# Router logits from transposed raw rows, and idle TensorE products between the first expert stage and the conv

## The chip, the cores and the metric

The kernel runs on one core of a Trainium2 chip (trn2). The metric is the device time of one execution in microseconds (us), as the median of several runs. TensorE multiplies matrices, VectorE and ScalarE work on vectors, GpSimd issues the indirect DMAs (gathers and scatters of rows), and SyncE issues nearly all other DMAs, in program order. The engines run independently and wait for one another through semaphores.

## The reference: what is computed

One inference step of a two-layer network over T = 544 frames (512 of a new stream, 32 of a running one) of D = 1024 features, all in fp32. Each layer is a mixer and a mixture of experts, each ahead of a residual addition and behind an RMS norm. The mixer of layer 0 is attention plus a gated recurrence, that of layer 1 a short convolution between two projections. The part that the change touches is the mixture's router:

```
def rmsnorm(x, gain):
    y = xf * rsqrt(mean(xf * xf, axis=-1) + RMS_EPS)
    return y * gain
hp = hp + mix_p
hp = hp + hier_moe(rmsnorm(hp, norm_ffn[layer]), w_group, b_group, w_expert, b_expert, w1, w3, w2)
...
g_logits = xt @ w_group + b_group                      # 4 groups
grp      = argmax(g_logits)                            # top-1 group
e_logits = xt @ w_expert + b_expert                    # 32 experts, 8 in a group
topv, topi = top_k(e_logits of grp, 2)                 # top-2 experts in it
h   = silu(xt @ w1[e]) * (xt @ w3[e]) * gate
out = h @ w2[e]
```

The normed row is the raw row times one number of the row (1/rms) times one gain per feature. A logit is a sum over features, so the gain can be multiplied into the router's weights and 1/rms can be applied to the finished sum.

## The kernel before

**Tiling.** The frames lie as five chunks of 128, 128, 128, 128 and 32 rows (`ROWS`) in `H`, one row to a partition, its features along the partition's memory. KT = 8 is the number of 128-feature pieces.

**Stages, in order of time.** Input projection and mixer of layer 0 (to about 299 us); its output projection (`project_out(0, ...)`, L909) to 360 us; the router of layer 0 to about 392 us; its 32 experts to 633 us; combining the experts' rows, the norm and the transposes for the conv to 664 us; the conv (`conv_terms`, L1044) to 813 us; the output projection of layer 1 to 871 us, its router to 901 us, its experts to 1137 us, and the combining and writing of the results to the end.

**Output projection and its additions.** `project_out` runs over four column quarters s and, in each, over the five chunks c, 24 products each. VectorE's `residual` adds each result to `H` (L1621). When the last quarter of a chunk is in, it signals `h_ok`, ScalarE's `square` takes the chunk's sum of squares (L1089) and its root (L1091), and VectorE's `norm` (L1351, L1357) takes the reciprocal into `rstd` and writes H * rstd * gain to `XF`, one chunk behind the additions. For the expert stages the row is written with its features permuted: feature 8q + k goes to column 128k + q, so that piece k is contiguous. Five DMAs (L428) copy `XF` to `x_rows` in DRAM, from which the experts' rows are gathered later.

**Router.** TensorE's `norm_transpose` (L648) transposes each chunk of `XF` in eight 128-column pieces into two PSUM banks: chunks 0, 1 and 2 behind the last quarter's products of chunks 2, 3 and 4, then chunks 3 and 4. ScalarE's `xt_copy` (L1099) copies the banks to `XT`, chunk 4's second half is copied by VectorE's `xt_high` (L1361). The logits (L931) are 16 products, `wr` (the router's weights of one piece, 36 columns) by 256 or 288 frames of `XT`. ScalarE (L1275) and VectorE (L1637) copy them out, TensorE turns them back to one frame a partition (L936), and VectorE adds the bias `biasr` (L1643, L1644). Then follow VectorE's choice of group and experts, products that rank the frames within each expert, the tables, and GpSimd's first gather (L584).

**Idle products.** `idle_products(b, count)` (L627) multiplies the identity by itself into PSUM bank b, count times, and nothing reads the result. Each layer's router has groups of 6, 26, 11 and 22 of them, each in a stretch in which TensorE waits.

**Expert weights.** The weights of an expert are 3 MB. Six sets fit in memory. SyncE loads experts 0 to 2 beside the output projection, experts 3 and 4 when the five `x_rows` writes have landed (`x_out`) and the logits are done (`lg_mm`; expert 3 goes where `XT` lies, experts 4 and 5 where `XN` and `XF` lie), expert 5 when the first two gathers have landed, and each later one when the expert six before it has been used. Experts are computed in pairs (L966, L972, L978, L983), and GpSimd scatters their rows to `y_rows` (L588).

**From layer 0's experts to the conv.** When all scatters have landed, SyncE loads the rows back into `yab` (L467), VectorE's `combine` adds them to `H` (L1791), and squares, norms (now to `XN`, not permuted), transposes (L648), and the split of each value into a high and a low part (`mixer_in_hi`, L1116; `mixer_in_lo`, L1369) follow for chunks 0 to 2. TensorE then starts the first feature block, 48 records in two of three parts, transposes chunks 3 and 4, and goes on with the rest. On its own side TensorE waits, after the last expert, for ScalarE's last copy of a result, reads the largest number of rows of an expert (`value_load`), and branches around a loop for experts with over 64 rows, which isn't taken here.

## Time and profile before

| | |
|---|---|
| median of 3 runs | 1168.28 us (1168.16 to 1169.54) |
| the profiled execution, its own time | 1169.81 us |
| its span | 1168.1 us |
| TensorE busy | 1013.1 us (87%) |
| VectorE, ScalarE, GpSimd busy | 389.6, 307.1, 189.8 us |
| memory traffic | 282.81 MB, mean 242 GB/s |
| chain that ended last | TensorE 64%, DMA 19%, SyncE's issues 9%, VectorE 5% |
| mean granted TensorE clock | 0.936 of full speed |

How to read it: the profile shows one execution, taken by the hardware. PE is TensorE, PEld its weight loads, DVE VectorE, ACT ScalarE, POOL GpSimd, SP SyncE (SPq: its issuing of DMAs). L909 is line 909 of the kernel. An fp32 product can stand as two records, since it is carried out in passes. Times of a row count from the start of the span. The releaser behind an idle time is inferred.

### The profile page before, as it was taken

The page shows a single profiled execution, that of the slowest core. Times are in us where ns is not written, and L with a number is a line of the kernel's source. Part 1 is how long each engine was busy: PE and PEld are TensorE (multiplying, and loading weights), DVE is VectorE, ACT ScalarE, POOL GpSimd, SP SyncE. Part 2 cuts the span into 40 slices and gives each one's busy share as a digit, 9 for nine tenths or more (in the row PEclk, how much of TensorE's full clock was granted, in tenths as well). Part 3 has the DMA queues.
Part 4 walks back from the last instruction along what each step waited for, and adds up shares of the span by engine and source line. Part 5 has one row for each costly group of instructions (what it writes and reads, how often), then busy time and mean ns, then how long its engine had stood idle before and what let it go on. Part 6 is the DMA issues. An engine that isn't in the chain of part 4 may idle for free.

```text
span 1168.1 us, 20266 instructions
## 1 busy us (share of the span) xinstructions
PE 1013.1 (87%) x8635; PEld 793.4 (68%) x8635; DVE 389.6 (33%) x857; ACT 307.1 (26%) x712; POOL 189.8 (16%) x188
## 2 busy tenths in 40 slices
PE   6999999989998899778775499999998999778880
PEld 5999898965897665444442499999996655444440
DVE  5242464257336211101101755546354111001104
ACT  6254344246223122111112421221131121111110
POOL 7344213120000122122111000000001222122110
PEclk9999998989899999989889599999999999899896
DMA  6432121420744999999996624243677999999966
GB/s 223 96 105 82 38 75 60 111 93 2 248 163 195 360 416 416 417 417 415 417 414 205 213 55 109 55 109 144 181 165 282 405 417 416 416 417 416 415 265 240
DMA packets 114724, 282.81 MB, mean 242 GB/s; under 512 B 22814, under 2 KB 69962, under 8 KB 98216
## 3 DMA queue, kind: packets, MB, share of 16 engines
q1 hardware_dynamic: 104904, 263.63, 60.8%
q0 software_dynamic: 9728, 17.85, 4.1%
q8 instruction: 70, 1.15, 0.5%
q14 instruction: 22, 0.18, 0.0%
HBM read 270.54 MB, written 27.02 MB: 255 GB/s over the span
## 4 chain that ended last, share of the span: by engine, by line
PE 64%; DMA 19%; SPq 9%; DVE 5%; issue 2%; ACT 1%; POOL 1%; DVEq 0%; POOLq 0%; ACTq 0%
DMA w<-in_w_dram 15%; PE banks L1044 13%; PE banks L972 10%; PE banks L677 10%; PE banks L909 9%; PE banks L676 6%; SPq L396 6%; PE banks L983 5%; SPq L399 2%; PE banks L648 1%; PE banks L966 1%; DMA yab<-y_rows 1%; PE banks L870 1%; PE banks L854 1%; PE banks L837 1%
## 5 line engine op out<-in xcount | busy, mean ns | idle before, releaser
L972 PE MATMUL banks<-w,xgT 128*64 128x256 f32 x2048 | 261.6, 416 | 65.5 <-DMA w<-in_w_dram 64.3
L972 PEld LDWEIGHTS banks<-w,xgT 128*64 128x64 f32 x2048 | 162.2, 150 | 172.4 <-DMA w<-in_w_dram 72.7
L1729 DVE TENSOR_TENSOR hh<-banks,sg 128x128 f32<-128x128 f32 x64 | 18.7, 292 | 407.0 <-ACT sg L1290 407.0
L588 POOL DMA_INDIRECT y_rows<-ys,yidx x64 | 63.6, 994 | 381.3 <-ACT ys L1298 379.9
L983 PE MATMUL banks<-w,hT 128*64 128x512 f32 x512 | 116.9, 598 | 0.0
L1044 PE MATMUL banks<-xc_hi,wc_hi 128*128 128x272 f32 x384 | 111.5, 290 | 2.1 <-DVE xc_lo L1369 2.1
L1044 PE MATMUL banks<-xc_hi,wc_lo 128*128 128x272 f32 x384 | 111.7, 291 | 0.0
L1044 PE MATMUL banks<-xc_lo,wc_hi 128*128 128x272 f32 x384 | 111.0, 289 | 0.0
L584 POOL DMA_INDIRECT xr<-x_rows,gidx x32 | 33.4, 1045 | 403.6 <-DVE yidx L1715 385.2
L574 POOL TENSOR_TENSOR wab_lo<-wab,wab_hi 128x512 fp32r<-128x512 f32 x56 | 77.0, 1406 | 131.4 <-ACT wab_hi L1104 130.5
L677 PE MATMUL banks<-wab_hi,xc_hi 128*128 128x256 f32 (+1 forms) x320 | 94.4, 295 | 3.8 <-DVE xp_lo L1369 2.1
L1290 ACT ACTIVATE sg<-banks 128x128 f32<-128x128 f32 x64 | 17.8, 278 | 293.0 <-PE banks L972 293.0
L677 PE MATMUL banks<-wab_hi,xp_lo 128*128 128x256 f32 (+1 forms) x320 | 93.0, 291 | 0.0
L677 PE MATMUL banks<-wab_lo,xc_hi 128*128 128x256 f32 (+1 forms) x320 | 90.4, 286 | 0.0
L1044 PEld LDWEIGHTS banks<-xc_hi,wc_hi 128*128 128x128 f32 x384 | 73.0, 190 | 2.6 <-issue 2.5
L983 PEld LDWEIGHTS banks<-w,hT 128*64 128x64 f32 x512 | 34.1, 136 | 58.5 <-issue 54.6
L1044 PEld LDWEIGHTS banks<-xc_lo,wc_hi 128*128 128x128 f32 x384 | 73.0, 190 | 0.0
L1044 PEld LDWEIGHTS banks<-xc_hi,wc_lo 128*128 128x128 f32 x384 | 72.8, 190 | 0.0
L1298 ACT ACTIVATE ys<-banks 128x512 f32<-128x512 f32 x64 | 38.2, 597 | 97.9 <-PE banks L983 97.9
L677 PEld LDWEIGHTS banks<-wab_hi,xc_hi 128*128 128x128 f32 (+1 forms) x320 | 58.3, 182 | 5.1 <-issue 4.2
L677 PEld LDWEIGHTS banks<-wab_hi,xp_lo 128*128 128x128 f32 (+1 forms) x320 | 58.3, 182 | 0.4
L677 PEld LDWEIGHTS banks<-wab_lo,xc_hi 128*128 128x128 f32 (+1 forms) x320 | 56.9, 179 | 0.7 <-POOL wab_lo L574 0.3
(284 smaller groups left out, 1762.0 us busy)
## 6 DMA issues: line engine op xcount, KB each, us to landing
w<-in_w_dram SPq DMA_DIRECT2D x192, 1024.0 KB, 23.0
wab<-in_w_in_ab_dram SPq DMA_DIRECT2D x13, 1024.0 KB, 5.1
wc<-in_w_in_c_dram SPq DMA_DIRECT2D x24, 512.0 KB, 5.8
yab<-y_rows SPq DMA_DIRECT2D x16, 512.0 KB, 6.7
wo<-in_w_out_ab_dram SPq DMA_DIRECT2D x4, 1024.0 KB, 7.0
x_rows<-XF SPq DMA_DIRECT2D x8, 512.0 KB, 3.5
wo<-in_w_out_c_dram SPq DMA_DIRECT2D x4, 1024.0 KB, 5.9
H<-in_x_prompt_dram SPq DMA_DIRECT2D x4, 512.0 KB, 8.3
```

The lines of the kernel that those rows point to most:

```text
L396: sp.dma_start(w13[s][:, part, :, :], w[l, bass.ds(e, 1)].rearrange("e (p k) f -> p (e k) f", p=P)).then_inc(done, 16)
L399: sp.dma_start(w2s[s][:], w2[l, bass.ds(e, 1)].rearrange("e (a p) n -> p (e a) n", p=P)).then_inc(done, 16)
L574: last = pool.tensor_tensor(wab_lo[n % 3][:, k:k + 2, :], wab[n % 3][:, k:k + 2, :], wab_hi[n % 3][:, k:k + 2, :].bitcast(F32), ALU.subtract)
L584: pool.indirect_dma_start(xr[i][:, :], None, x_dram[l][:, :], bass.IndirectOffsetOnAxis(ap=index.bitcast(U32), axis=0), bounds_check=T - 1 ...
L588: pool.indirect_dma_start(y_dram[l][:, :], bass.IndirectOffsetOnAxis(ap=index.bitcast(U32), axis=0), ys[i][:, :], None, bounds_check=4 * T ...
L676: return pe.matmul(out, w[:, k, cols], x[:, k, t], **flags)
L677: return pe.matmul(out, x[:, k, t], w[:, k, :], **flags)
L909: last = pe.matmul(bank[i % 4][0:ROWS[c], 0:OW], z(a, k)[:, c * P:c * P + ROWS[c]], w(b, k, s), start=k == 0 and j == 0, stop=k == KT - 1 ...
L972: last = pe.matmul(bank[hb][64 * f:64 * f + 64, 0:2 * P].rearrange("p (w j) -> p w j", w=2), xgT[i][:, k, 64 * ab:64 * ab + 64], w13[s][:, ...
L983: last = pe.matmul(bank[6 + ab][64 * n:64 * n + 64, :], hT[ab][:, 64 * f:64 * f + 64], w2s[s][:, f, n * 512:(n + 1) * 512], start=f == 0, ...
L1044: last = pe.matmul(bank[3 * half + a][:, 0:HALF], w[s][:, k, a, :], x[:, k, half * HALF:(half + 1) * HALF], start=k == 0 and j == 0, stop= ...
L1298: act.activation(ys[e % 4][:], bank[6 + ab][:, :], ACT.Copy).then_inc(ys_ok, 1)
```

## The change

In both layers the router's logits are taken from transposed raw rows. `norm_transpose` with an odd n waits for `h_ok` in place of `xn_ok` and loads columns k, k+8, k+16, ... of `H`. It is moved one chunk forward: chunks 0 to 3 stand behind the products of chunks 1 to 4. The six idle products before chunk 4 are gone. ScalarE makes all the copies to `XT`, and those of chunks 3 and 4 stand ahead of chunk 4's square; VectorE's `xt_high` is gone. VectorE multiplies `wr` by the gains (`gcol`, a new DMA) once a layer, ahead of the first addition. The logits' products run first over the frames of chunks 0 and 1, then over those of chunks 2 to 4, with a signal of their own for the first part. The bias addition becomes a scaled one, by `rstd`, chunk by chunk. SyncE issues expert 3's load when the logits are done, and only expert 4's also waits for the `x_rows` writes. `XF` is still made and written as before. Apart from the router, TensorE runs 140 idle products between layer 0's last expert and the first transposes for the conv, and 10, 4 and 12 behind those of chunks 0, 1 and 2.

```
+        gcol = small("gcol", KT)
...
                 sp.dma_start(wr[:, :, NG:NR], w_expert[l].rearrange("(p k) n -> p k n", p=P)).then_inc(wr_in, 16)
                 sp.dma_start(biasr[:, 0:NG], b_group[l:l + 1, :].partition_broadcast(P)).then_inc(wr_in, 16)
                 sp.dma_start(biasr[:, NG:NR], b_expert[l:l + 1, :].partition_broadcast(P)).then_inc(wr_in, 16)
+                sp.dma_start(gcol[:], norm_ffn[l].rearrange("(p k) -> p k", k=KT)).then_inc(wr_in, 16)
 
 
             wcv = w_in_c[0].rearrange("(k p) (a m n) -> a m p k n", p=P, a=3, n=P)
...
                 for c in range(NC):
                     sp.wait_ge(xn_ok, NC * (2 * l + 1) + c + 1)
                     sp.dma_start(x_dram[l][c * P:c * P + ROWS[c], :], XF[0:ROWS[c], c, :]).then_inc(x_out, 16)
+                sp.wait_ge(lg_mm, 2 * l + 1)
+                first_load(l, 3)
                 sp.wait_ge(x_out, 16 * NC * (l + 1))
-                sp.wait_ge(lg_mm, 2 * l + 1)
-                for j in (3, 4):
-                    first_load(l, j)
+                first_load(l, 4)
                 for i in range(2):
                     sp.wait_ge(xr_in[i], 16 * (PAIRS // 2 * l + 1))
                 first_load(l, 5)
...
                     pe.matmul(bank[b][:, 0:P], ident[:], ident[:], start=True, stop=True)
 
             def norm_transpose(n, c):
-                if n % 2 == 1 and c == 4:
-                    idle_products(1, 6)
-                pe.wait_ge(xn_ok, NC * n + c + 1)
+                if n % 2 == 0:
+                    pe.wait_ge(xn_ok, NC * n + c + 1)
+                else:
+                    pe.wait_ge(h_ok, NC * (n - 1) + c + 1)
                 if n == 0 and c == 0:
                     pe.wait_ge(pool_c, zeroed[0])
 
...
                         pe.wait_ge(xt_a if half == 0 else xt_d, NC * n + c - 1)
                     for kk in range(4):
                         k = 4 * half + kk
-                        last = pe.transpose(bank[low + half][:, kk * P:kk * P + ROWS[c]], (XN, XF)[n % 2][0:ROWS[c], c, k * P:(k + 1) * P],
+                        rows = H[0:ROWS[c], c, k::KT] if n % 2 else XN[0:ROWS[c], c, k * P:(k + 1) * P]
+                        last = pe.transpose(bank[low + half][:, kk * P:kk * P + ROWS[c]], rows,
                                             ident[0:ROWS[c], 0:ROWS[c]])
                     last.then_inc(xt_mm, 1)
 
...
                             last = pe.matmul(bank[i % 4][0:ROWS[c], 0:OW], z(a, k)[:, c * P:c * P + ROWS[c]], w(b, k, s),
                                              start=k == 0 and j == 0, stop=k == KT - 1 and j == 2)
                     last.then_inc(op_mm, 1)
-                    if s == OQ - 1 and c >= 2:
-                        norm_transpose(2 * n + 1, c - 2)
+                    if s == OQ - 1 and c >= 1:
+                        norm_transpose(2 * n + 1, c - 1)
 
             def z_ab(part, k):
                 return ((zA_hi, zA_lo), (zB_hi, zB_lo))[k // 4][part][:, k % 4, :]
...
             project_out(0, z_ab, lambda part, k, s: (wo_hi, wo_lo)[part][0][s][:, k, :], w_lo, 15)
 
             def mixture(l):
-                for c in (3, 4):
-                    norm_transpose(2 * l + 1, c)
-                pe.wait_ge(xt_a, NC * (2 * l + 2))
-                pe.wait_ge(xt_d, NC * (2 * l + 2))
+                norm_transpose(2 * l + 1, NC - 1)
                 pe.wait_ge(op_add, OQ * NC * (l + 1))
-
-                pe.wait_ge(wr_in, 64 * (l + 1))
-                for k in range(KT):
-                    for p0, t in ((0, slice(0, 2 * P)), (64, slice(2 * P, T))):
+                pe.wait_ge(wg_ok, l + 1)
+                for p0, t, chunks, done in ((0, slice(0, 2 * P), 2, lgh_mm), (64, slice(2 * P, T), NC, lg_mm)):
+                    pe.wait_ge(xt_a, NC * (2 * l + 1) + chunks)
+                    pe.wait_ge(xt_d, NC * (2 * l + 1) + chunks)
+                    for k in range(KT):
                         last = pe.matmul(bank[0][p0:p0 + NR, 0:t.stop - t.start], wr[:, k, :], XT[l][:, k, t], start=k == 0, stop=k == KT - 1)
-                last.then_inc(lg_mm, 1)
+                    last.then_inc(done, 1)
                 pe.wait_ge(lgT_ok, 2 * l + 2)
                 for c in range(NC):
                     p0, t0 = (0, c * P) if c < 2 else (64, (c - 2) * P)
...
             def frames_ready(c):
                 pe.wait_ge(xt_a, NC * 2 + c)
                 pe.wait_ge(xt_d, NC * 2 + c)
+            idle_products(2, 140)
             for c in range(3):
                 norm_transpose(2, c)
+                idle_products(2, (10, 4, 12)[c])
             pe.wait_ge(wc_lo_ok, 1)
             frames_ready(3)
             for a in range(3):
...
                 for q in range(1, OQ):
                     out_hi(l, q)
                 for c in range(NC):
+                    if c == NC - 1:
+                        xt_copy(2 * l + 1, c - 1, 0, xt_a)
+                        xt_copy(2 * l + 1, c - 1, 1, xt_d)
+                        xt_copy(2 * l + 1, c, 0, xt_a)
+                        xt_copy(2 * l + 1, c, 1, xt_d)
                     square(2 * l + 1, c)
-                    if c >= 2:
-                        xt_copy(2 * l + 1, c - 2, 0, xt_a)
-                        xt_copy(2 * l + 1, c - 2, 1, xt_d)
-                xt_copy(2 * l + 1, 3, 0, xt_a)
-                xt_copy(2 * l + 1, 3, 1, xt_d)
-                xt_copy(2 * l + 1, 4, 0, xt_a)
-                act.wait_ge(lg_mm, 2 * l + 1)
+                    if 0 < c < NC - 1:
+                        xt_copy(2 * l + 1, c - 1, 0, xt_a)
+                        xt_copy(2 * l + 1, c - 1, 1, xt_d)
+                act.wait_ge(lgh_mm, l + 1)
                 act.activation(lgT[0:NR, 0:2 * P], bank[0][0:NR, 0:2 * P], ACT.Copy).then_inc(lgT_ok, 1)
                 act.wait_ge(ge_ok, 2 * l + 1)
                 act.activation(rt[3][:, :, 0:NG], rt[3][:, :, 0:NG], ACT.Exp).then_inc(ex_ok, 1)
...
-
-            def xt_high(n, c):
-                dve.wait_ge(xt_mm, NXT * n + 2 * c + 2)
-                dve.tensor_copy(XT[n // 2][:, 4:8, c * P:c * P + ROWS[c]],
-                                bank[7 - 2 * (c % 2)][:, :].rearrange("p (k t) -> p k t", k=4)[:, :, 0:ROWS[c]]).then_inc(xt_d, 1)
...
 
             def residual(n):
 
+                dve.wait_ge(wr_in, 80 * (n + 1))
+                dve.tensor_tensor(wr[:], wr[:], bc(gcol[:].unsqueeze(2), [P, KT, NR]), ALU.mult).then_inc(wg_ok, 1)
                 for i in range(OQ * NC):
                     s, c = divmod(i, NC)
                     dve.wait_ge(op_mm, OQ * NC * n + i + 1)
...
                         if c > 0:
                             norm(2 * n + 1, c - 1)
                 norm(2 * n + 1, NC - 1)
-                xt_high(2 * n + 1, NC - 1)
             residual(0)
 
             def route(l):
...
                 dve.wait_ge(lg_mm, 2 * l + 1)
                 dve.tensor_copy(lgT[64:64 + NR, :], bank[0][64:64 + NR, 0:T - 2 * P]).then_inc(lgT_ok, 1)
                 dve.wait_ge(lg_mm, 2 * l + 2)
-                dve.wait_ge(wr_in, 64 * (l + 1))
                 z = [b[:, 0:NC * NR].rearrange("p (c n) -> p c n", c=NC) for b in (bank[2], bank[3])]
-                for i in range(2):
-                    c2 = slice(2 * i, 2 * i + 2)
-                    tie(dve.tensor_tensor(lg[:, c2, :], z[i][:, c2, :], bc(biasr[:].unsqueeze(1), [P, 2, NR]), ALU.add))
-                dve.tensor_tensor(lg[0:DEC, 4, :], z[1][0:DEC, 4, :], biasr[0:DEC, :], ALU.add).then_inc(lg_ok, 1)
+                for c in range(NC):
+                    n = ROWS[c]
+                    last = dve.scalar_tensor_tensor(lg[0:n, c, :], z[c // 2 if c < 4 else 1][0:n, c, :], rstd[0:n, c:c + 1], biasr[0:n, :], ALU.mult, ALU.add)
+                last.then_inc(lg_ok, 1)
                 dve.wait_ge(lg_ok, l + 1)
 
                 def first_max(v, w, rev, eq, key, hot, top):
```

On TensorE, the end of layer 0's output projection up to its router's first idle products. `wo_*` and `z*` are operands of the projection, `lgT` are the logits with the frames along the columns. Before:

```order
L909 MATMUL banks<-wo_lo_3_191,zB_hi 32x256
L648 MATMUL banks<-ident,XF 128x128 x16
L627 MATMUL banks<-ident 128x128 x6
L648 MATMUL banks<-ident,XF 128x32 x8
L931 MATMUL banks<-XT_104,wr 36x256
L931 MATMUL banks<-XT_104,wr 36x288
...
L936 MATMUL banks<-ident,lgT 128x36 x4
L936 MATMUL banks<-ident,lgT 32x36
L627 MATMUL banks<-ident 128x128 x26
```

And with the change:

```order
L913 MATMUL banks<-wo_lo_3_192,zB_hi 32x256
L652 MATMUL banks<-ident,H 128x128 x8
L652 MATMUL banks<-ident,H 128x32 x8
L933 MATMUL banks<-XT_105,wr 36x256 x8
L933 MATMUL banks<-XT_105,wr 36x288 x8
L938 MATMUL banks<-ident,lgT 128x36 x4
L938 MATMUL banks<-ident,lgT 32x36
L629 MATMUL banks<-ident 128x128 x26
```

One chunk's transposes are left behind the last product where two were (the other chunk's, and so each earlier one's, has moved a product forward), they read `H`, and six idle products are gone.

On ScalarE, the same place, from the square of chunk 2 to the copy of the logits (`junk,ssq` and `rms` are a chunk's square and root). Before:

```order
L1089 ACTIVATE junk,ssq<-H 128x1024
L1091 ACTIVATE rms<-ssq,epsc 128x1
L1099 ACTIVATE XT_104<-banks 128x4x128 x2
L1089 ACTIVATE junk,ssq<-H 128x1024
L1091 ACTIVATE rms<-ssq,epsc 128x1
L1099 ACTIVATE XT_104<-banks 128x4x128 x2
L1089 ACTIVATE junk,ssq<-H 128x1024
L1091 ACTIVATE rms<-ssq,epsc 128x1
L1099 ACTIVATE XT_104<-banks 128x4x128 x4
L1099 ACTIVATE XT_104<-banks 128x4x32
L1275 ACTIVATE lgT<-banks 36x256
```

And with the change, from the square of chunk 3:

```order
L1093 ACTIVATE junk,ssq<-H 128x1024
L1095 ACTIVATE rms<-ssq,epsc 128x1
L1103 ACTIVATE XT_105<-banks 128x4x128 x4
L1103 ACTIVATE XT_105<-banks 128x4x32 x2
L1093 ACTIVATE junk,ssq<-H 128x1024
L1095 ACTIVATE rms<-ssq,epsc 128x1
L1281 ACTIVATE lgT<-banks 36x256
```

The copies of the last chunks have moved ahead of chunk 4's square and root.

On TensorE, between the branch behind layer 0's experts and the conv. Before:

```order
L1021 COMPARE_AND_BRANCH
L1021 UNCONDITIONAL_BRANCH
L648 MATMUL banks<-ident,XN 128x128 x24
L1044 MATMUL banks<-xc_hi,wc_hi_265 128x272
L1044 MATMUL banks<-xc_lo,wc_hi_265 128x272
```

And with the change:

```order
L1023 COMPARE_AND_BRANCH
L1023 UNCONDITIONAL_BRANCH
L629 MATMUL banks<-ident 128x128 x140
L652 MATMUL banks<-ident,XN 128x128 x8
L629 MATMUL banks<-ident 128x128 x10
L652 MATMUL banks<-ident,XN 128x128 x8
L629 MATMUL banks<-ident 128x128 x4
L652 MATMUL banks<-ident,XN 128x128 x8
L629 MATMUL banks<-ident 128x128 x12
L1046 MATMUL banks<-xc_hi,wc_hi_266 128x272
```

Nothing is moved here; 166 products are put in, in TensorE's own order.

## Rows read from the trace of the kernel before

**Rows 1.** the page, section 2: memory traffic in 40 equal slices of the span

```profile
GB/s 223 96 105 82 38 75 60 111 93 2 248 163 195 360 416 416 417 417 415 417 414 205 213 55 109 55 109 144 181 165 282 405 417 416 416 417 416 415 265 240
```

**Rows 2.** windows around the first gather: busy per engine, TensorE clock, DMA share, GB/s

```profile
390.00:392.00 2.00, 0.37 (x3) 0.37 (x4) 0.00 (x0) 0.00 (x0) 0.00 (x0) 1.00 0.30 113
394.00:396.00 2.00, 2.00 (x22) 1.60 (x19) 0.00 (x0) 0.22 (x1) 0.48 (x1) 1.00 0.94 385
```

**Rows 3.** chain of waits, end of the output projection: start us, us, what

```profile
356.23 0.87 PE banks L648 x8
357.10 2.79 PE banks L909 x24
```

**Rows 4.** timeline of TensorE, layer 0's router: start us, us, line, operation [idle before]

```profile
363.64 2.73 PE L627 MATMUL banks<-ident 128*128 128x128 f32 x12
366.31 0.99 PE L648 MATMUL banks<-ident,XF 32*128 32x32 f32 x8
367.72 4.08 PE L931 MATMUL banks<-XT,wr 128*36 128x256 f32 x32 [0.43 <-ACT XT L1099]
```

**Rows 5.** timeline of VectorE, the same stretch

```profile
349.10 0.42 DVE L1621 TENSOR_TENSOR H<-banks,H 128x256 f32<-128x256 f32 x1 [2.43 <-PE banks L909]
...
359.91 0.41 DVE L1621 TENSOR_TENSOR H<-banks,H 32x256 f32<-32x256 f32 x1 [0.78 <-PE banks L909]
...
362.72 2.03 DVE L1357 SCALAR_TENSOR_TENSOR XF<-H,rstd,gffn 128x1024 f32<-128x1024 f32 x1
...
371.91 0.46 DVE L1637 COPY lgT<-banks 36x288 f32<-36x288 f32 x1 [4.10 <-PE banks L931]
372.82 0.50 DVE L1643 TENSOR_TENSOR lg<-banks,biasr 128x72 f32<-128x72 f32 x2 [0.45 <-PE banks L936]
```

**Rows 6.** timeline of ScalarE, the same stretch

```profile
358.17 1.07 ACT L1099 ACTIVATE XT<-banks 128x512 f32<-128x512 f32 x2
360.41 1.06 ACT L1089 ACTIVATE junk<-H 128x1024 bf16<-128x1024 f32 x1 [1.18 <-DVEq L1626]
...
361.59 0.29 ACT L1091 ACTIVATE rms<-ssq,epsc 128x1 f32<-128x1 f32 x1
```

**Rows 7.** timeline of VectorE, layer 1's router

```profile
871.26 0.41 DVE L1621 TENSOR_TENSOR H<-banks,H 32x256 f32<-32x256 f32 x1 [0.78 <-PE banks L909]
...
881.72 0.46 DVE L1637 COPY lgT<-banks 36x288 f32<-36x288 f32 x1 [4.10 <-PE banks L931]
```

**Rows 8.** timeline of GpSimd, the first gather of layer 0

```profile
385.98 1.20 POOL L584 DMA_INDIRECT xr<-x_rows,gidx  x1 [124.98 <-DVE yidx L1715]
```

**Rows 9.** timeline of TensorE: two groups of idle products in layer 0's router

```profile
372.71 6.07 PE L627 MATMUL banks<-ident 128*128 128x128 f32 x52
...
379.74 2.70 PE L627 MATMUL banks<-ident 128*128 128x128 f32 x22
```

**Rows 10.** timeline, all engines, from layer 0's last expert to the conv

```profile
635.20 2.76 ACT L1314 ACTIVATE wc_hi<-wc 128x3072 fp32r<-128x3072 f32 x1 [1.46 <-DMA wc<-in_w_in_c_dram]
...
654.32 1.97 PE L648 MATMUL banks<-ident,XN 128*128 128x128 f32 x8 [21.23 <-DVE XN L1357]
...
662.81 1.29 DVE L1369 TENSOR_TENSOR xc_lo<-banks,xc_hi 128x512 fp32r<-128x512 f32 x2 [0.42 <-ACT xc_hi L1116]
...
671.14 1.28 DVE L1357 SCALAR_TENSOR_TENSOR XN<-H,rstd,gmix 128x1024 f32<-128x1024 f32 x1
```

**Rows 11.** chain of waits, start of the conv

```profile
664.25 7.73 PE banks L1044 x48
...
673.46 139.09 PE banks L1044 x1104
```

**Rows 12.** a window in that stretch, columns as in rows 2

```profile
636.00:640.00 4.00, 0.00 (x0) 0.00 (x0) 2.00 (x1) 1.96 (x1) 0.00 (x0) 0.59 1.17 316
```

**Rows 13.** groups by form, VectorE, 374 to 376 us: count | busy, mean ns | idle

```profile
L1661 DVE TENSOR_REDUCE rt<-rt 128x40 f32<-128x160 f32 x1 | 0.4, 433 | 0.0
L1659 DVE TENSOR_TENSOR rt<-lg,rt 128x160 f32<-128x160 f32 x1 | 0.3, 318 | 0.0
```

More of the change, by code:

```diff
@@ L118, in hmoe_step @@
         biasr = small("biasr", NR)
+        gcol = small("gcol", KT)
         row_no = small("row_no", 2 * NC)
@@ L416, in router_load @@
                 sp.dma_start(biasr[:, NG:NR], b_expert[l:l + 1, :].partition_broadcast(P)).then_inc(wr_in, 16)
+                sp.dma_start(gcol[:], norm_ffn[l].rearrange("(p k) -> p k", k=KT)).then_inc(wr_in, 16)
             wcv = w_in_c[0].rearrange("(k p) (a m n) -> a m p k n", p=P, a=3, n=P)
@@ L428, in mixture @@
                     sp.dma_start(x_dram[l][c * P:c * P + ROWS[c], :], XF[0:ROWS[c], c, :]).then_inc(x_out, 16)
+                sp.wait_ge(lg_mm, 2 * l + 1)
+                first_load(l, 3)
                 sp.wait_ge(x_out, 16 * NC * (l + 1))
-                sp.wait_ge(lg_mm, 2 * l + 1)
-                for j in (3, 4):
-                    first_load(l, j)
+                first_load(l, 4)
                 for i in range(2):
@@ L629, in norm_transpose @@
             def norm_transpose(n, c):
-                if n % 2 == 1 and c == 4:
-                    idle_products(1, 6)
-                pe.wait_ge(xn_ok, NC * n + c + 1)
+                if n % 2 == 0:
+                    pe.wait_ge(xn_ok, NC * n + c + 1)
+                else:
+                    pe.wait_ge(h_ok, NC * (n - 1) + c + 1)
                 if n == 0 and c == 0:
@@ L647, in norm_transpose @@
                         k = 4 * half + kk
-                        last = pe.transpose(bank[low + half][:, kk * P:kk * P + ROWS[c]], (XN, XF)[n % 2][0:ROWS[c], c, k * P:(k + 1) * P],
+                        rows = H[0:ROWS[c], c, k::KT] if n % 2 else XN[0:ROWS[c], c, k * P:(k + 1) * P]
+                        last = pe.transpose(bank[low + half][:, kk * P:kk * P + ROWS[c]], rows,
                                             ident[0:ROWS[c], 0:ROWS[c]])
@@ L911, in project_out @@
                     last.then_inc(op_mm, 1)
-                    if s == OQ - 1 and c >= 2:
-                        norm_transpose(2 * n + 1, c - 2)
+                    if s == OQ - 1 and c >= 1:
+                        norm_transpose(2 * n + 1, c - 1)
             def z_ab(part, k):
@@ L921, in mixture @@
             def mixture(l):
-                for c in (3, 4):
-                    norm_transpose(2 * l + 1, c)
-                pe.wait_ge(xt_a, NC * (2 * l + 2))
-                pe.wait_ge(xt_d, NC * (2 * l + 2))
+                norm_transpose(2 * l + 1, NC - 1)
                 pe.wait_ge(op_add, OQ * NC * (l + 1))
-                pe.wait_ge(wr_in, 64 * (l + 1))
-                for k in range(KT):
-                    for p0, t in ((0, slice(0, 2 * P)), (64, slice(2 * P, T))):
+                pe.wait_ge(wg_ok, l + 1)
+                for p0, t, chunks, done in ((0, slice(0, 2 * P), 2, lgh_mm), (64, slice(2 * P, T), NC, lg_mm)):
+                    pe.wait_ge(xt_a, NC * (2 * l + 1) + chunks)
+                    pe.wait_ge(xt_d, NC * (2 * l + 1) + chunks)
+                    for k in range(KT):
                         last = pe.matmul(bank[0][p0:p0 + NR, 0:t.stop - t.start], wr[:, k, :], XT[l][:, k, t], start=k == 0, stop=k == KT - 1)
-                last.then_inc(lg_mm, 1)
+                    last.then_inc(done, 1)
                 pe.wait_ge(lgT_ok, 2 * l + 2)
@@ L1266, in mixture @@
                 for c in range(NC):
[L1267 to L1274 removed]
+                    if c == NC - 1:
+                        xt_copy(2 * l + 1, c - 1, 0, xt_a)
+                        xt_copy(2 * l + 1, c - 1, 1, xt_d)
+                        xt_copy(2 * l + 1, c, 0, xt_a)
+                        xt_copy(2 * l + 1, c, 1, xt_d)
+                    square(2 * l + 1, c)
+                    if 0 < c < NC - 1:
+                        xt_copy(2 * l + 1, c - 1, 0, xt_a)
+                        xt_copy(2 * l + 1, c - 1, 1, xt_d)
+                act.wait_ge(lgh_mm, l + 1)
                 act.activation(lgT[0:NR, 0:2 * P], bank[0][0:NR, 0:2 * P], ACT.Copy).then_inc(lgT_ok, 1)
@@ L1615, in residual @@
             def residual(n):
+                dve.wait_ge(wr_in, 80 * (n + 1))
+                dve.tensor_tensor(wr[:], wr[:], bc(gcol[:].unsqueeze(2), [P, KT, NR]), ALU.mult).then_inc(wg_ok, 1)
                 for i in range(OQ * NC):
@@ L1629, in residual @@
                 norm(2 * n + 1, NC - 1)
-                xt_high(2 * n + 1, NC - 1)
             residual(0)
@@ L1638, in route @@
                 dve.wait_ge(lg_mm, 2 * l + 2)
-                dve.wait_ge(wr_in, 64 * (l + 1))
                 z = [b[:, 0:NC * NR].rearrange("p (c n) -> p c n", c=NC) for b in (bank[2], bank[3])]
-                for i in range(2):
-                    c2 = slice(2 * i, 2 * i + 2)
-                    tie(dve.tensor_tensor(lg[:, c2, :], z[i][:, c2, :], bc(biasr[:].unsqueeze(1), [P, 2, NR]), ALU.add))
-                dve.tensor_tensor(lg[0:DEC, 4, :], z[1][0:DEC, 4, :], biasr[0:DEC, :], ALU.add).then_inc(lg_ok, 1)
+                for c in range(NC):
+                    n = ROWS[c]
+                    last = dve.scalar_tensor_tensor(lg[0:n, c, :], z[c // 2 if c < 4 else 1][0:n, c, :], rstd[0:n, c:c + 1], biasr[0:n, :], ALU.mult, ALU.add)
+                last.then_inc(lg_ok, 1)
                 dve.wait_ge(lg_ok, l + 1)
```

15 lines of the change are left out of this document (3 added, 12 removed).

## The prediction, made before the changed kernel was run

> **What bounds the kernel now.** I read the page first, for the traffic in forty slices, then the chain of waits, then timelines of the three places that the diff touches. The traffic row [rows 1] stands at 414 to 417 GB/s in slices 15 to 21 (some 409 to 613 us) and at 405 to 417 again in slices 32 to 38 (905 to 1110 us): both expert stages are bound by the stream of expert weights. What starts that stream decides when a stage ends. At 390 to 392 us traffic is down to 113 GB/s, at 394 to 396 it is back at 385 [rows 2]: experts 3 and 4 have been loaded, and SyncE waits for the first gather before it issues expert 5. So a router that finishes earlier moves the gather and the whole saturated stream, and the stage ends earlier by as much. Between the stages the bound is TensorE: from 673.46 us the conv's products run for 139.09 us without a break [rows 11]. Whatever delays that run lengthens the kernel one for one.
>
> **Part one, the router.** I rebuild layer 0 from its rows. Now: the last product of the projection (chunk 4) is added at 359.91, chunk 4's normed row is ready at 362.72 + 2.03 = 364.75 [rows 5], the six idle products still run until 366.3 at the low clock (12 records in 2.73 us, against 52 in 6.07 [rows 4, 9]), chunk 4's transposes and their copies follow, the logits take 4.08 us from 367.72 [rows 4], and the copy of the logits ends at 371.91 + 0.46 = 372.37 [rows 5].
>
> After: chunk 1's product ends at about 348.9, since its addition starts at 349.10 [rows 5]. Behind it TensorE runs transposes, product, three times over: 3 x (0.87 + 2.8) [rows 3] gives chunk 4's product ending at 359.9. That is where it ends today, within 0.3 us: the third set of transposes that now precedes it takes the place of the wait for chunk 0's normed row. Chunk 3's transposes end at 360.8. Chunk 4's follow its addition (0.41) and take 0.5, half of the 0.99 at the half clock [rows 4], to 361.3. ScalarE copies a half chunk in 0.53 [rows 6]: chunk 3 by 361.7, chunk 4 by 362.1. Then it squares chunk 4, 360.41 to 361.88 today, so 1.47 us [rows 6], to 363.6. The logits need only the copies: 361.3 + 4.08 = 365.4. VectorE is last: chunk 4's row waits for that root, 363.6 + 0.2 + 2.03 = 365.8, clearing lg 0.2, the copy 0.46, and so 366.5. **Gain 5.9 us**; what is late next is this normed row, no longer TensorE.
>
> Off it go 0.2 us, because five scaled additions of some 0.18 stand for the three that took 0.50 and one more [rows 5], and 0.2 for the transposes' new operand (below). Layer 0 nets 5.5. In layer 1 the clock did not fall, so the same stretch is shorter today: from the addition at 871.26 to 882.18 [rows 7]. After, the addition starts 0.3 later and 6.4 later the copy is done, at 878.0: 4.2, less 0.4, nets 3.8. From there to the gather's issue (385.98 us [rows 8], 13.2 us behind 372.82) nothing is changed, and the x_rows writes that also gate it end well before: the last row is ready at 365.8, some 15 us ahead of the gather's new issue. Expert 3 no longer waits for these writes, expert 4 still does; both issue earlier than today's.
>
> Costs at nothing: gcol's DMA is one more issue before layer 0's projection; the scaling of wr on VectorE sits ahead of the first addition, and TensorE needs that addition three products later (3 x 2.8 us); only beyond that would it be felt. In layer 1 both are done long before.
>
> The bounds of part one are the operand. Transposes now load H with a step of 32 bytes. No row shows TensorE doing that. The nearest rows are VectorE's: a reduce that reads 160 elements a 32-byte step apart takes 433 ns, a tensor operation over 160 contiguous ones 318 [rows 13], so 0.72 ns more an element. One load of 128 would take 0.09 us more, a set of eight 0.74. Five sets lie on the path, 3.7 us a layer. The lower end is zero, since a set of chunk 4, with as many columns to load but only 32 to stream, runs in 0.5 where a full one takes 0.87 [rows 3, 4]: the load has room beside the stream. I take 0.2. The Trainium skill (SBUF — State Buffer, Door 1: The DMA port swizzle, the note on SBUF cachelines) says that accesses that cross to a new 16-byte line each pay a penalty; with fp32 at a step of eight every element would do so. By it the sum would be rival B's; no row of TensorE here shows it.
>
> **Part two, the idle products.** One product is two records: 52 records for 26 products in 6.07 us, 22 for 11 in 2.70 [rows 9]. Their spacing is 0.112 us by the difference, (6.07 - 2.70) / 30, and 0.117 by 6.07 / 52; I take 0.1135, so a product costs 0.227 at full clock. TensorE is free when ScalarE has copied the last result, 635.20 - 1.46 = 633.74, and has then to read the count and branch; ScalarE, which does the same, resumes at 635.20 at the latest [rows 10]. I take 635.0 (bounds 633.8 and 636.5). 140 products take 31.8 us and end at 666.8. But today chunk 0's transposes start at 654.32 [rows 10]: **the products overrun the wait by 12.5 us.** Only some 85 would fit.
>
> Then, in order: transposes 0.87, ten products 2.3, transposes 0.87, four 0.9, transposes 0.87, twelve 2.7. The conv starts at 675.3 instead of 664.25. The first 48 conv records then run at full clock, 48 x 0.126 = 6.05 instead of 7.73 [rows 11], to 681.35. Next are the transposes of chunks 3 and 4. VectorE made chunk 4's row 8.3 us after the split of chunk 2 (662.81 + 1.29 = 664.10, to 672.42 [rows 10]). That split now ends at 674.6, hence 682.9, and the run resumes at about 683.7 instead of 673.46. **Cost 10.2 us.** Bounds: 8.5 with an early branch, 12 with a late one or with the clock low at first.
>
> **Sum.** -5.5 + 10.2 - 3.8 = +0.9 us. The profiled execution took 1169.81 (span 1168.1), so it would take 1170.7; the median of the three runs is 1168.28, so I predict **1169.2**. A measurement of this kernel tells about 0.2% (2.3 us) from no change: gain and loss nearly cancel.
>
> **Rivals.** A, the forecast: 0.48; its own range 1165 to 1173, from the bounds above (about 0.06 of it faster by over 0.2%, 0.32 within, 0.10 slower).
>
> B, slower: the strided loads of H cost VectorE's 0.72 ns an element. 2 x 3.7 - 0.4 = 7.0 more, 1176.2. It decides from 0.14 us a set of eight, (2.3 - 0.9) / 10. For: the nearest rows. Against: the room beside the stream. 0.20, nearly all slower.
>
> C: the clock. TensorE idles over a microsecond before the products, and today, left idle, it has a mean clock of 0.59 at 636 to 640 [rows 12]. If it falls as the products start and stays down for some 3.3 us, 1.7 us are lost: 1170.9. If it stayed low throughout, 32 more. 0.10, of it 0.06 slower.
>
> D, faster: a product costs half of what I count, so 15.9 us, over at 650.9, before the transposes' 654.32. Nothing is delayed and the conv gains some 1.5 us by the clock: 1168.3 - 9.3 - 1.5 = 1157.5. Against it: the 52 records [rows 9]. 0.08. The Trainium skill (TensorE: Matmul & The Clock Gate, Back-to-back issue gap) gives about 81 ns per matmul at 128 columns, by which 140 take 11 us and this rival would hold; this trace's 0.227 us speaks against it.
>
> E: the expert stages do not pass the router's gain on, as other traffic sets the stream's end: +10.2 alone, 1178.5. Against: the gap before the saturated stretch [rows 2]. 0.07, slower.
>
> F: the opposite; expert 3's earlier load closes part of that gap, up to 2.8 us a layer: 1163.6. 0.07, faster.
>
> Faster 0.06 + 0.08 + 0.07 = 0.21; within 0.2% 0.32 + 0.04 = 0.36; slower 0.10 + 0.20 + 0.06 + 0.07 = 0.43. The range 1163 to 1178 leaves out D, E and the end of C, under 2 in 10.
>
> **What would show it.** In the profile after: the logits' copy 6.4 us behind chunk 4's addition in both layers; 280 records of idle products ahead of the conv, some 0.114 apart, and transposes at about 667; the unbroken conv run 10 us further behind the last expert than today; no half-clock stretch there. Wrong: transposes of H spaced well over 0.11 us (B), products over before the transposes' rows are ready (D), or expert stages that last longer by the router's gain (E).

## The result, and the profile after

| | us | 95% interval of the ratio |
|---|---|---|
| before, median of 20 runs | 1168.80 (1166.64 to 1173.60) | |
| changed, median of 20 runs | 1172.72 (1170.45 to 1178.88) | 1.0037 [1.0025, 1.0048] |

The change costs 3.9 us, or 0.37%: slower by more than the 0.2% bound, if little. The profiled execution (1178.88 us, span 1177.2) is the longest of the twenty. Its expert stages happened to be long (last expert's copy 249.5 us behind the gather in layer 0 and 248.2 in layer 1, before 247.8 and 245.6), so I compare distances between events, not times on the axis.

First the router, in the changed kernel's chain of waits (start us, us, what), layer 0. L652, L913, L933 are the old L648, L909, L931; L1639 the old L1637.

```profile
349.14 0.90 PE banks L652 x8
350.04 2.86 PE banks L913 x24
...
357.58 2.73 PE banks L913 x24
360.31 1.87 PE banks L652 x16
362.19 6.64 PE banks L933 x32
...
368.92 0.47 DVE lgT L1639
...
369.82 0.90 DVE lg L1644 x5
```

A set of eight strided transposes takes 0.90 us against 0.87 [rows 3]. But the 32 records of the logits take **6.64 us where they took 4.08** [rows 4]. VectorE's timeline (start, us, line, operation) says who is last now:

```profile
364.09 2.01 DVE L1363 SCALAR_TENSOR_TENSOR XF<-H,rstd,gffn 128x1024 f32<-128x1024 f32 x1
366.07 0.21 DVE L1637 MEMSET lg<- 128x180 f32 x1
368.92 0.46 DVE L1639 COPY lgT<-banks 36x288 f32<-36x288 f32 x1 [2.64 <-PE banks L933]
...
880.70 0.41 DVE L1624 TENSOR_TENSOR H<-banks,H 32x256 f32<-32x256 f32 x1 [0.77 <-PE banks L913]
...
889.27 0.46 DVE L1639 COPY lgT<-banks 36x288 f32<-36x288 f32 x1 [2.64 <-PE banks L933]
```

Chunk 4's normed row is done at 366.1. VectorE clears `lg` and then stands idle for 2.64 us, in both layers, until TensorE has the logits. What differs is their order. Before, each feature's weights served rows 0 to 255 and then the rest, so the two output groups (partitions 0 to 35, 64 to 99) took turns. The change runs all eight features into the first group and then all into the second. Windows of 0.4 us with the logits' products alone, changed kernel (first the bounds and the length, then busy time and the number of records on PE and on PEld; third from last the granted clock):

```profile
362.80:363.20 0.40, 0.40 (x3) 0.22 (x2) 0.00 (x0) 1.00 0.00 0
...
364.80:365.20 0.40, 0.40 (x6) 0.29 (x6) 0.00 (x0) 1.00 0.97 399
365.20:365.60 0.40, 0.40 (x6) 0.27 (x3) 0.00 (x0) 1.00 0.14 51
...
367.20:367.60 0.40, 0.40 (x3) 0.22 (x2) 0.00 (x0) 1.00 0.68 154
```

And one of the kernel before:

```profile
368.20:368.60 0.40, 0.40 (x7) 0.38 (x5) 1.00 0.00 0
```

The clock is full (1.00) throughout. Three or four records are in work at some time of each 0.4 us, but six where one group follows the other; in the kernel before it is six to eight in most windows.

Then TensorE's timeline ahead of the conv (L629 is the old L627):

```profile
633.97 31.53 PE L629 MATMUL banks<-ident 128*128 128x128 f32 x280 [1.94 <-issue]
665.34 1.04 PE L652 MATMUL banks<-ident,XN 128*128 128x128 f32 x8
666.21 2.40 PE L629 MATMUL banks<-ident 128*128 128x128 f32 x20
...
680.18 1.09 PE L652 MATMUL banks<-ident,XN 128*128 128x128 f32 x8 [0.21 <-DVE XN L1363]
681.64 0.68 PE L652 MATMUL banks<-ident,XN 32*128 32x32 f32 x8 [0.36 <-DVE XN L1363]
```

140 products take 31.53 us. Chunk 0's row was ready at 653.6 by VectorE's timeline, its transposes start at 665.34, the conv's unbroken run at 682.31, by the chain.

Where the time went (us between events; the last expert's copy is ScalarE's L1304, before L1298):

| stretch | before | changed |
|---|---|---|
| layer 0: chunk 4's last but one addition to its last | 16.51 | 16.88 |
| layer 0: chunk 4's last addition to the gather's issue | 26.07 | 22.81 |
| gather to the last expert's copy | 247.77 | 249.52 |
| last expert's copy to the conv's unbroken run | 39.71 | 49.63 |
| layer 1: chunk 4's last but one addition to its last | 16.24 | 16.88 |
| layer 1: chunk 4's last addition to the gather's issue | 24.43 | 22.73 |
| layer 1: gather to the last expert's copy | 245.58 | 248.20 |

The last addition now comes 0.4 and 0.6 us later, with one more set of transposes ahead of it, and the gather 3.3 and 1.7 us nearer to it. So the router gives 2.9 and 1.1 us, the conv's stretch costs 9.9: +5.9 by one profile each, +3.9 by the medians.

### The profile page after: what moved, and what is told of

Same layout as the page of the kernel before. It is cut to its first block, busy times and chain, and to the rows that moved or that the text cites. A ratio compares the mean times of both kernels' runs of the same rounds, so it can differ in the third digit from the quotient of the medians.

```text
span 1177.2 us, 20888 instructions
## 1 busy us (share of the span) xinstructions
PE 1047.9 (89%) x8943; PEld 824.5 (70%) x8943; DVE 390.6 (33%) x861; ACT 307.2 (26%) x714; POOL 190.0 (16%) x188
## 4 chain that ended last, share of the span: by engine, by line
PE 64%; DMA 15%; SPq 14%; DVE 4%; issue 2%; ACT 1%; POOL 0%; DVEq 0%; POOLq 0%; ACTq 0%
DMA w<-in_w_dram 13%; PE banks L1046 12%; PE banks L681 10%; PE banks L913 10%; SPq L397 9%; PE banks L974 9%; PE banks L680 6%; SPq L400 4%; PE banks L985 4%; PE banks L629 3%; PE banks L652 1%; PE banks L874 1%; PE banks L858 1%; PE banks L933 1%; PE banks L841 1%
## 5 line engine op out<-in xcount | busy, mean ns | idle before, releaser
L629 PE MATMUL banks<-ident 128*128 128x128 f32 x568 | 65.6, 276 | 1.9 <-issue 1.9
L629 PEld LDWEIGHTS banks<-ident 128*128 128x128 f32 x568 | 64.2, 192 | 2.9 <-issue 2.8
L1304 ACT ACTIVATE ys<-banks 128x512 f32<-128x512 f32 x64 | 38.2, 597 | 97.8 <-PE banks L985 97.8
```

What stands on the lines that cost most here:

```text
L629: pe.matmul(bank[b][:, 0:P], ident[:], ident[:], start=True, stop=True)
L1304: act.activation(ys[e % 4][:], bank[6 + ab][:, :], ACT.Copy).then_inc(ys_ok, 1)
```

## The experiments

Theory: the logits' order costs some 2 us a layer, and idle products that do not fit cost 0.225 us each. Rivals: the strided loads or the new data make the logits slow; the expert stages take gains back; the products are harmless. "Changed" in a diff is the changed kernel. Runs of one table stood beside the kernel before on the same chip.

**First four: the parts apart.** One run has 80 products for 140:

```
-            idle_products(2, 140)
+            idle_products(2, 80)
```

> The changed kernel with 80 idle products in place of 140 before chunk 0's transposes (10, 4 and 12 kept). Theory (overrun): the 140 held chunk 0's transposes back by 11 us; 80 products take 80 x 0.225 = 18.0 us from some 1.3 us behind the last expert's copy and end before the row is ready. The conv's long run then starts 9.9 + 1.5 us closer to the last expert than with 140 (1.5 us closer than in the kernel before, since the clock stays up): 11 us less than the changed kernel, about 1161.5 us. Rival (the length hardly matters, the wait for VectorE's rows sets the conv's start): within 2 us of the changed kernel, 1171 to 1173.

One restores the order of the logits and keeps all else:

```
-                for p0, t, chunks, done in (...):
-                    for k in range(KT):
+                for k in range(KT):
+                    for p0, t, done in (...):
```

> The changed kernel with the logits' products alternating between the two groups of frames, as before the change, in place of one group after the other (all of them then wait for all copies). Theory (the order of the products costs): the 32 records go from 6.64 us back to about 4.1, start 0.4 us later, and the copy of the logits ends about 2.1 us earlier in each layer: 4.2 us less than the changed kernel, 1168.5. Rival (the 6.64 us are due to the earlier place or to the raw rows' copies, not to the order): records stay at 0.2 us apart and the time at 1172.7.

One is the kernel before, with `idle_products(2, 140)` and the 10, 4 and 12 added:

> The kernel before with only the 140 + 10 + 4 + 12 idle products put in. Theory: the conv's long run starts 49.6 us behind the last expert's copy where it was 39.7: +9.9 us, about 1178.7. Rival (part of the cost is given back by the clock or by the expert stage of layer 1): +4 us or less.

One is the changed kernel with those four calls removed, so the router alone:

> The changed kernel without any of the 166 idle products ahead of the conv: the router's part alone. Theory (by the two profiles): the gather goes out 2.9 us earlier in layer 0 and 1.1 us in layer 1, both carried to the end: 4.0 us less than before, 1164.8; together with +9.9 that gives +5.9, which is above the +3.9 measured, so a part may be larger or smaller by 2. Rival (the stream of weights does not pass the gain on): 1168.8, as before. Rival (the earlier load of expert 3 gives more): 1162 to 1163.

"Gather behind addition" is the stretch from chunk 4's last addition to the gather's issue, "conv run behind last expert" the one from the last expert's copy to the conv's unbroken run, each by that run's profile.

| run | us | ratio to before (1168.43) | gather behind addition, layers 0, 1 | conv run behind last expert |
|---|---|---|---|---|
| 80 products | 1166.04 | 0.9974 [0.9960, 0.9988] | 22.82, 22.73 | 40.50 |
| alternating | 1170.97 | 1.0024 [1.0010, 1.0039] | 20.73, 20.64 | 51.27 |
| idle products only | 1178.57 (4 runs) | 1.0098 [1.0082, 1.0113] | 24.53, 24.43 | 49.80 |
| router only | 1164.92 | 0.9972 [0.9959, 0.9985] | 22.82, 22.73 | 42.17 |

The parts come out as I expected: +10.1 for the products, -3.5 for the router. Their sum, 6.6, is not 3.9. Some of it may have a row: with the router only, the conv's unbroken run started 20.2 us behind chunk 0's transposes, before 19.1, and its first 48 records took 8.76 us where they took 7.73, as the clock stayed low longer; with the 140 products it is 17.0. That is one profile each, and the rest I leave open.

80 products gave 6.7 us back by the medians (7.4 by the ratios, each to its own runs of before), fewer than the 11 that I had expected and than the 9.1 by which the conv's run came nearer; this stays open. Alternating gave its 2.1 us in each layer, but only 1.75 in the time (1.5 by the ratios). Its profile shows one loss: the clock fell just after the products had begun, rival C, at a price of 33.16 - 31.53 = 1.6 us. Chain and windows (third from last: granted clock) of that run:

```profile
360.27 4.09 PE banks L933 x31
...
626.88 33.16 PE banks L629 x280
```
```profile
628.00:630.00 2.00, 2.00 (x14) 2.00 (x13) 0.20 (x1) 1.76 (x1) 0.00 (x0) 0.59 1.19 303
630.00:632.00 2.00, 2.00 (x12) 2.00 (x12) 2.00 (x1) 0.00 (x0) 0.00 (x0) 0.56 1.16 325
632.00:634.00 2.00, 2.00 (x21) 2.00 (x20) 1.15 (x1) 0.00 (x0) 0.00 (x0) 1.00 0.10 24
```

Of the nine profiles with such products, it fell at their start in two (this one and, further on, the one with none between the transposes: 80 took 19.76 us where they otherwise took 18.13). Whether that is why alternating gave so little isn't shown. The order paid more with fewer products, as the next four runs show.

**Next four: the remedies together, the order alone, the stride alone.** With both edits at once:

> The changed kernel with both remedies at once: 80 idle products in place of 140, and the logits' products taken feature by feature, alternating between the two output groups, as the kernel before has them. Theory (the two costs lie in different stretches and add): 1166.0 of the run with 80 products, less 2.1 us in each of the two router stretches, as the run with alternating products alone showed there: 1161.8; the last expert to the conv's unbroken run about 40.5 us. Rival (the two are not independent, since the next expert stage takes back what the router gives, as its time alone fell only by 1.75 us for 4.2 expected): 1164.3.

Alternating, without the idle products:

> The router's part alone, with alternating logits' products and no idle products ahead of the conv. Theory: 1164.9 of the run without idle products, less 4.2: 1160.7; the conv's run starts about 42.2 us behind the last expert. If 80 idle products are worth 1.6 us by the clock, as the marks say (40.5 against 42.2), this run is above the one with 80 and alternating products; if they are worth nothing, as the times 1166.0 against 1164.9 of the two runs without alternation say, it is 1 us below. Rival on the order (half of the gain is taken back): 1163.2.

The kernel before with its two loops over features and groups exchanged:

```
-                for k in range(KT):
-                    for p0, t in ((0, slice(0, 2 * P)), (64, slice(2 * P, T))):
+                for p0, t in ((0, slice(0, 2 * P)), (64, slice(2 * P, T))):
+                    for k in range(KT):
```

> The kernel before with one edit: its logits' products are issued half by half, first all of rows 0 to 255 into one output group, then the rest into the other, in place of alternating. Theory (the order alone makes 32 records take 6.6 us instead of 4.1): 2.5 us more in layer 0 and in layer 1, 1173.4, and records of the logits some 0.2 us apart. Rival (the 6.6 us come from the strided operands or the new data, not from the order): records as before in 4.1 us and the time unchanged, 1168.4.

The changed kernel with adjacent features (the layout `(k p)` for `w_group`, `w_expert` and `norm_ffn` to match):

```
-                        rows = H[0:ROWS[c], c, k::KT] if n % 2 else XN[...]
+                        rows = (XN, H)[n % 2][0:ROWS[c], c, k * P:(k + 1) * P]
```

> The changed kernel with features in their natural order: the transposes load 128 adjacent elements of H, and the router's weights and gains are loaded from DRAM with rows 128 apart to match. Theory (the 32-byte step costs TensorE next to nothing): a set of eight transposes takes 0.87 us instead of 0.90, and the time is that of the changed kernel, 1172.7, within 1 us. Rival (the step costs VectorE's 0.72 ns an element somewhere that the sets' rows do not show): some 7 us less, 1165.7. If loading the gains with scattered 4-byte elements delays the first products, layer 0 starts later by what its row shows.

| run | us | ratio to before (1170.08) | gather behind addition | conv run behind last expert |
|---|---|---|---|---|
| 80, alternating | 1161.47 (6 runs) | 0.9914 [0.9890, 0.9939] | 20.73, 20.64 | 40.34 |
| none, alternating | 1160.26 (6 runs) | 0.9927 [0.9906, 0.9947] | 20.73, 20.64 | 39.31 |
| before, group by group | 1172.96 | 1.0034 [1.0016, 1.0052] | 27.12, 27.03 | 40.22 |
| adjacent features | 1171.35 | 1.0015 [1.0002, 1.0029] | 22.43, 22.35 | 49.63 |

The third run settles the cause: with the old operands and the old data, the exchange alone makes the logits slow. TensorE's timeline of it, layers 0 and 1, and then of the kernel before in layer 1:

```profile
365.03 6.67 PE L931 MATMUL banks<-XT,wr 128*36 128x256 f32 x32 [0.43 <-ACT XT L1099]
...
877.09 6.67 PE L931 MATMUL banks<-XT,wr 128*36 128x256 f32 x32 [0.43 <-ACT XT L1099]
```
```profile
877.53 4.08 PE L931 MATMUL banks<-XT,wr 128*36 128x256 f32 x32 [0.43 <-ACT XT L1099]
```

It costs 2.6 us in layer 1. In layer 0 only 1.05 of it shows against the profile of before, because there the clock fell ahead of chunk 4's transposes [rows 4] and here it did not. It did not in the run with the idle products only either, whose router is the old one: against its 24.53 us the exchange costs 2.6 in layer 0 too. (The time rose by 2.9 us, with an interval of 1.9 to 6.1.) So 1.5 of the 26.07 us before, and of the 3.3 us gained in layer 0, belong to a fall of the clock that came in one of the three profiles in which the transposes stand as before. Put right, the order gives 4.6 us (1166.04 to 1161.47 and 1164.92 to 1160.26; 7 and 5 by the ratios, as the kernel before read 1.7 us higher on this chip), where the marks say 4.2. Both remedied versions beat both kernels. The Trainium skill (TensorEngine Tiling (Array Packing), Tiling Modes) says that different tiles of the array can load weights and multiply in parallel. The trace agrees in kind: 0.128 us a record in turns (4.08 / 32), 0.208 in sequence (6.64 / 32), 1.6 times. But no row names a tile, and the exchange does two things at once: in turns, consecutive products write different output groups, and they also use the same weights. Weight loads are not saved by that (32 of 113 ns each, in both orders), yet no run separates the two.

The stride is priced by the last run. Chain of the kernel with adjacent features:

```profile
347.83 0.87 PE banks L653 x8
...
358.93 1.49 PE banks L653 x16
360.42 6.64 PE banks L934 x32
```

0.03 us less in a set of full chunks, but 0.38 less over the sets of chunks 3 and 4 (1.87 to 1.49), nearly all of it in chunk 4's. TensorE's groups by shape in 345 to 372 us (count, then busy us and mean ns of one), first changed, then adjacent:

```profile
L652 PEld LDWEIGHTS banks<-ident,H 128*128 128x128 f32 x32 | 3.9, 193 | 0.0
L652 PE MATMUL banks<-ident,H 32*128 32x32 f32 x8 | 1.1, 272 | 0.0
```
```profile
L653 PEld LDWEIGHTS banks<-ident,H 128*128 128x128 f32 x32 | 3.6, 140 | 0.0
L653 PE MATMUL banks<-ident,H 32*128 32x32 f32 x8 | 0.7, 224 | 0.0
```

So a strided load does take longer, 193 ns where an adjacent one takes 140, and this shows where only 32 columns stream beside it; beside 128 it is almost covered. The gather comes 0.38 us nearer to the addition in each layer, and the addition 0.07 nearer to the one before it. The ratios differ by more, 1.0037 and 1.0015, from two sets of runs; I read no more from them than that B's 7 us are not there. The Trainium skill (SBUF — State Buffer, Door 1: The DMA port swizzle) has each crossing to a new 16-byte line pay. The trace agrees that it costs something, 0.053 us a load by the loads (193 - 140 ns) and 0.048 by the products where little covers it (272 - 224), which is about half of rival B's 0.09.

**Last four: how many products.** 110, alternating:

> The changed kernel with alternating logits' products and 110 idle products ahead of the conv, between the 80 and the 140 tried so far. Theory (about 85 fit, every one beyond costs 0.225 us on the path): the 110 end some 26.1 us behind the last expert's copy, where chunk 0's row is ready 19 to 22 us behind it, so chunk 0's transposes start 3 to 6 us late and the conv's run 43 to 44 us behind the last expert; the time is some 3 us above that of 80 products (1164.5 against 1161.5). Rival (only the end counts, not how many): the time of 80 products.

80, with none between the transposes:

> Alternating logits' products, 80 idle products ahead of the conv and none between the transposes of chunks 0 to 2. Theory (the conv's unbroken run waits for the normed rows of chunks 3 and 4, which VectorE makes at its own pace, so the 26 between cost nothing and give nothing once the clock is up): the conv's run 40.3 us behind the last expert and the time of 80 products with them, 1161.5. Rival (without them the clock falls again in the waits between the transposes): the granted clock is 0.5 again within the stretch, the run starts 42 us behind the last expert, as without idle products.

And none against 80 once more, on one chip:

> The same kernel as the router's part with alternating products and no idle ones, beside the next run on one chip, since the profiles say that 80 idle products bring the conv's run 1.7 us nearer to the chunk that starts it (18.5 against 20.2) and the times of the runs do not show it. Theory (the clock's gain is real, but expert stages vary by more than it): 1160.5, and 1.7 us above the run with 80. Rival (the gain is given back elsewhere): no difference, or below it by 1 us.

> The same kernel as the one with 80 idle products and alternating logits' products, beside the run before this one on the same chip. Theory: 1.7 us less than without idle products, 1158.8. Rival: the same as it or 1 us more, 1160.5 to 1161.5.

| run, all alternating | us | ratio to before (1169.11) | conv run behind last expert |
|---|---|---|---|
| 110 products | 1165.32 (11 runs) | 0.9967 [0.9953, 0.9982] | 42.95 |
| 80, none between | 1162.55 (6 runs) | 0.9947 [0.9931, 0.9964] | 39.01 |
| none, again | 1162.26 (6 runs) | 0.9939 [0.9922, 0.9956] | 40.71 |
| 80, again | 1161.79 (6 runs) | 0.9938 [0.9920, 0.9956] | 38.68 |

(A twelfth run of 110 products took 5604.51 us, for a reason that nothing here shows, and is left out.) 110 overrun chunk 0's row by 5.93 us and cost 3.5 against 80 (1165.32 and 1161.79). From 110 to 140 the conv's run moves by 49.63 - 42.95 = 6.68, and 30 x 0.225 = 6.75. So the price of each product too many is shown. Without products between the transposes the clock falls again, as the rival of that run said; its windows:

```profile
654.00:656.00 2.00, 1.22 (x9) 0.98 (x10) 1.97 (x4) 1.99 (x5) 0.00 (x0) 1.00 0.24 33
656.00:658.00 2.00, 1.66 (x8) 1.25 (x8) 2.00 (x4) 1.15 (x3) 0.00 (x0) 0.53 0.17 12
658.00:660.00 2.00, 0.24 (x1) 0.27 (x2) 1.89 (x4) 0.29 (x1) 0.00 (x0) 0.50 0.80 73
```

The conv's run was nevertheless no later behind chunk 0's transposes (18.1 us, against 18.2 and 18.5). With the clock low, its first 48 records took 7.73 us and now stand in the chain that ended last, but they began 8.9 us behind chunk 0's transposes and not 9.4 to 9.9, as with the products between; and with those products the run would wait for VectorE all the same (below). In this profile the products between are neither gain nor loss.

**80 against none stays a draw.** Pairs of medians: +1.1, +1.2, -0.5 us for 80. Yet the conv's run starts 18.2, 18.5 and 18.2 us behind chunk 0's transposes with 80, and 20.2, 20.2 and 18.8 without (in the last of these the clock rose within 656 to 658 us, in the first two only after 662). 80 do not always keep it up either: in the profile with 18.5 it fell in the wait between the last of the 80 and chunk 0's row, and was 0.50 from 650 to 652 us. VectorE caps that gain. In the chain of the first run with 80, in the changed kernel's order, the conv's run waits for VectorE's rows of chunks 3 and 4:

```profile
666.05 1.28 DVE XN L1363
...
667.51 1.30 DVE XN L1363
668.80 0.04 issue
668.85 0.68 PE banks L652 x8
669.52 20.56 PE banks L1046 x162
```

The 1 to 2 us that are left are smaller than what expert stages vary by (layer 1's lasted from 244.0 to 248.4 us over these profiles), and than the time from the last expert to chunk 0's transposes where these start on time (19.1 to 22.3). Whether 80 products give back elsewhere what they gain is open.

## Why the prediction was right and where not

- **The range held** (1163 to 1178), and slower, the likeliest of the three outcomes at 0.43, is what came. The forecast itself, 1169.2, by which gain and loss "nearly cancel", was 3.5 us too low. That the range covered it is partly luck: its upper part was there for rival B and the branch, not for what came, and the profiles' marks add up to +5.9, the parts' own runs to +6.6, of which the whole showed only 3.9, for reasons that stay open.
- **The step that failed:** "The logits need only the copies: 361.3 + 4.08 = 365.4". I carried the 4.08 us of the old order [rows 4] over to a new one; they take 6.64. With it falls "VectorE is last ... no longer TensorE": VectorE was done when I said (row at 366.1, said 365.8) and then waited 2.64 us. The copy ended at 369.4, not 366.5, and 9.0 us behind chunk 4's addition in both layers, not 6.4. My range had no bound for this term, and no rival. The rest of the gain's mechanism was right: alternating, the stretch from addition to gather falls by 26.07 - 20.73 = 5.3 and 24.43 - 20.64 = 3.8.
- Smaller steps: the last addition came 0.4 us later in layer 0, where I had it "within 0.3 us" and counted nothing, and 0.6 in layer 1, where I said 0.3. With both, the router gave 2.9 and 1.1 us, not 5.5 and 3.8. And the low clock ahead of chunk 4's transposes, of which I counted the end as gain, is not in every execution: without it, layer 0 gains 1.5 less.
- A smaller size: chunk 4's transposes, "0.5, half of the 0.99 at the half clock", took some 1.0 with the stride. "I take 0.2" for the stride should have been 0.4 to 0.5 a layer (0.38 + 0.07). The argument against rival B, room beside the stream, is shown for full sets, but chunk 4's set had too little room. B's 7 us did not come.
- **Part two held.** 0.227 us a product (0.225), start 635.0 behind a copy done at 633.74, 1.3 us (1.29), overrun 12.5 (11.8), cost 10.2 (9.9 by the marks, 10.1 by its own run). Also "only some 85 would fit": 80 were done in time where the clock stayed up, 110 were 5.9 us late, which puts the limit at 84 in that run.
- Rival C's fall of the clock was seen, in two other runs' profiles, for 1.6 us where I gave it 1.7. D is out: 31.53 us for 140. The Trainium skill (TensorE: Matmul & The Clock Gate, Back-to-back issue gap) has about 81 ns a matmul of 128 columns; these fp32 products, of two records each, took 225 (31.53 / 140). E is out: the router alone gained 3.5 us in the time. F is out: from the gather to the last expert's copy it is 247.9 us in layer 0 and 246.0 in layer 1 in the mean of the eleven profiles with the new router, 247.9 and 245.9 in the three with the old one, in either order.

## What to carry to other kernels

A duration read from a trace belongs to an order of instructions as much as to their shapes. When a change swaps two loops, price the new neighbours: here, products that wrote one output group to its end took 1.6 times as long as the same products in turns. Filler work that keeps an engine awake has a length of its own: divide the shortest wait by the measured price of one, stay below it, and check first that the wake-up is worth anything; here no count that was tried (80, 110, 140) was measurably better than none.

## What the runs showed of the hardware that I had not expected

- fp32 products with 36 output rows took 0.128 us a record when they alternated between output partitions 0 and 64, and 0.208 when they did not, at the same full clock. Weights, operands, results and the number of weight loads were the same.
- A weight load with a 32-byte step took 193 ns, an adjacent one 140. Of that, 0.004 us showed beside a stream of 128 columns (0.90 against 0.87 for eight) and 0.05 beside one of 32.
- Without idle products, the moment at which the clock rose varied: in two profiles of one kernel it came some 8 and some 16 us behind chunk 0's transposes. The conv's unbroken run started 18.8 and 20.2 us behind them.
